# Splits and sums of the next block placed between the additions of the down product, in a one-core streaming trunk layer

## The chip, the core and the metric

The kernel runs on one core of one Trainium2 chip. PE is TensorE, DVE is VectorE, ACT is ScalarE, SP issues the DMAs. Each engine works through its own list of instructions in the order in which they are written, and waits at semaphores for the others. The metric is the device time of one execution in microseconds. All matrix products are made in three matmuls of fp32r pieces: a number is split into a high part (a copy by ACT) and a low part (a difference by DVE), and high x high, high x low and low x high are summed.

## What is computed

One layer for 17 tiles of 128 rows (2048 prompt rows, 128 sample rows), width 1024, d_ff 2816:

```python
h = rms_norm(x, norm1); p = h @ w_in                       # token mixing: gMLP and gated DeltaNet
x = x + jnp.concatenate([y_a, y_b], axis=-1) @ w_o
h2 = rms_norm(x, norm2)
x = x + (jax.nn.silu(h2 @ w_gate) * (h2 @ w_up)) @ w_down
y = rms_norm(x, final_norm)
```

Beside y the layer returns the recurrent states and the last rows of the convolution and of v.

## The kernel before

It has two phases, one program each, with a barrier between them.

**The mixing** (`prompt_phase`) runs tile by tile. Between the small steps of tile t, every engine works off quarters of the large products in step with a common counter (`upto(t, stop)`, with `SLOT` = 32 quarters a tile). Quarter functions also finish the first 12 tiles (`DONE`) as far as the next phase needs them: `scale_rows` (DVE) scales a row tile by its norm, `turn_h2` (PE) transposes its two halves into the bank `gs`, `h2_columns` (DVE) scales them out of PSUM, `store_h2` (SP) stores them. `output(t)` (DVE) forms the mixed tile. At the end SP loads the last weight piece of the next phase (`a["ahead"][-1]`, w_up) into room that row tiles used, stores the state and the last mixed tile, and waits for all of it.

**The feed-forward phase** (`out_phase`) holds three groups of 6, 6 and 5 tiles and runs 11 blocks of 256 columns of d_ff for each: `B` = 0 to 32. Blocks 0, 11 and 22 open a group. Block 10 is called `switch` in the code, block 22 is `BEFORE`. gate and up are computed in a Winograd form of Strassen's algorithm: seven products for each side, 14 in a block (`one_product`, 12 matmuls of 384 or 320 columns each). Their weight pieces go through a ring of five slots: `ring_hi(B, i)` (ACT) and `ring_lo(B, i)` (DVE) split piece i. Four of the seven need sums of quarter blocks, `sum1` to `sum4` (DVE), made in place in `sums`, so sum 2 comes after the pieces of sum 1 have been split. Piece 4 of the next block needs sum 2.

The order of a block's products is A11, S1, S2, S3, A12, A22, S4 (in blocks 0 and 22 A11, A12, S1, S2, S3, A22, S4), each for gate and up. `seed` and `keep_u2` (ACT) carry sums from bank to bank between the products, `keep_p5` saves one. Four results of a block are formed by `corner`, `gate` (ACT), `product`, `out_hi` (ACT) and `out_lo` (DVE).

The down phase follows: 12 (in the last group 10) halves `down_half`, six matmuls of 512 columns each, into four banks in turn. `add_half(B, i)` (DVE) adds half i to `acc`. Half i waits for addition i - 4; half 0 waits for the third `out_lo` of the block. The weights of the down product come as two halves of 512 KB through one buffer: `load_down_half` (SP) waits for `down_half_lo` of the one before.

At the end of a group, `y_factor(gi, t)` (ACT) waits for the additions of tile t and forms its norm, `write_y` (DVE) scales the rows, `store_y` and `load_x` (SP) exchange them for the next group's. At the `switch` the operands of the next group (`operand_hi`, ACT, and `operand_lo`, DVE, seven of 1536 columns) are split between these steps.

Before block 22 comes the output projection of the last group, `last_norms` with `scale_tile`, `turn` (PE), `take_turned` and `early_piece` for its five tiles, and `last_t(i)`, the sums of its operands.

The order of every engine is written out by hand. In the kernel before, the pieces and sums of block B + 1 stand between the four results of block B.

## Time and profile before

| | us |
|---|---|
| median of 3 runs | 2684.31 |
| lowest, highest run | 2680.48, 2686.01 |
| the profiled execution | 2679.19 |
| its span (first to last instruction) | 2677.4 |
| PE busy | 2595.4 |
| DVE busy | 1833.9 |
| ACT busy | 1220.5 |
| DMA, mean | 122 GB/s |

The feed-forward phase begins at 1134.7 us of the span. Read the busy shares first, then who waited for whom on PE, and then the timeline at the places where it waited. A duration in the timeline is that of one instruction; on DVE and ACT the next one may begin a little before the end of the last. In the timeline a block shows neither its number nor the helper's name, only the helper's line: L3090 is `add_half`, L2926 `ring_lo`, L2933 `sum1`, L2938 `sum2`, L2945 `sum3`, L3078 `out_lo`, L2966 and L2962 `operand_lo`, L3129 `take_turned`, L3120 `scale_tile`, L2648 `ring_hi`, L2684, L2688 and L2682 `operand_hi`, L2695 `seed`, L2702 `keep_u2`, L2656 `down_half_hi`, L1171 `h2_columns`, L1399 `scale_rows`.

### The profile page before, as it was taken

The page shows a single profiled execution, that of the slowest core. Times are in us where ns is not written, and L with a number is a line of the kernel's source. Part 1 is how long each engine was busy: PE and PEld are TensorE (multiplying, and loading weights), DVE is VectorE, ACT ScalarE, POOL GpSimd, SP SyncE. Part 2 cuts the span into 40 slices and gives each one's busy share as a digit, 9 for nine tenths or more (in the row PEclk, how much of TensorE's full clock was granted, in tenths as well). Part 3 has the DMA queues.
Part 4 walks back from the last instruction along what each step waited for, and adds up shares of the span by engine and source line. Part 5 has one row for each costly group of instructions (what it writes and reads, how often), then busy time and mean ns, then how long its engine had stood idle before and what let it go on. Part 6 is the DMA issues. An engine that isn't in the chain of part 4 may idle for free.

```text
span 2677.4 us, 47276 instructions
## 1 busy us (share of the span) xinstructions
PE 2595.4 (97%) x18469; PEld 2282.2 (85%) x18469; DVE 1833.9 (68%) x3335; ACT 1220.5 (46%) x2267; POOL 28.1 (1%) x72
## 2 busy tenths in 40 slices
PE   8999999999999999689999999999999998999998
PEld 7878777777787777589999999899999997999997
DVE  4666767677677666587676668667666658677766
ACT  3435655655655656344242436324242435434444
POOL 1000000000000000000000000000000000000000
PEclk9999999999999999899999999999999998999999
DMA  9355444454444547433232325413131251222331
GB/s 310 101 157 174 143 131 131 142 155 115 158 145 117 206 150 245 165 131 114 72 118 71 103 75 186 134 49 94 48 95 48 88 172 48 87 65 86 95 87 56
DMA packets 372255, 325.67 MB, mean 122 GB/s; under 512 B 13985, under 2 KB 314130, under 8 KB 369986
## 3 DMA queue, kind: packets, MB, share of 16 engines
q1 hardware_dynamic: 371650, 322.63, 39.1%
q8 instruction: 148, 2.42, 0.4%
q14 instruction: 73, 0.60, 0.1%
q0 software_dynamic: 384, 0.02, 0.0%
HBM read 261.09 MB, written 61.51 MB: 120 GB/s over the span
## 4 chain that ended last, share of the span: by engine, by line
PE 51%; DVE 4%; ACT 1%; issue 1%; DMA 1%; SPq 0%; DVEq 0%; ACTq 0%
PE down_ps L3316 8%; PE down_ps L3317 8%; PE down_ps L3318 8%; PE up_ps L3322 3%; PE gate_ps L3322 3%; PE up_ps L3321 3%; PE gate_ps L3323 3%; PE gate_ps L3321 3%; PE up_ps L3323 3%; PE down_ps L3322 1%; PE down_ps L3321 1%; PE down_ps L3323 1%; PE gate_ps L3316 1%; PE gate_ps L3318 1%; PE gate_ps L3317 1%; PE up_ps L3317 1%
## 5 line engine op out<-in xcount | busy, mean ns | idle before, releaser
L1673 PE MATMUL pr_p<-hT_hi_p,w_hi_p 128*128 128x512 f32 x992 | 420.0, 423 | 2.1 <-ACT w_in_sb L747 1.1
L1675 PE MATMUL pr_p<-hT_hi_p,w_lo_p 128*128 128x512 f32 x992 | 389.4, 393 | 0.0
L1674 PE MATMUL pr_p<-hT_lo_p,w_hi_p 128*128 128x512 f32 x992 | 389.2, 392 | 0.0
L3090 DVE TENSOR_TENSOR middle<-down_ps,middle 128x512 f32<-128x512 f32 x374 | 257.6, 691 | 174.3 <-PE down_ps L3318 172.0
L3316 PE MATMUL down_ps<-wd_hi,act_hi 128*128 128x512 f32 x748 | 293.0, 392 | 9.8 <-DVE act_lo L3078 9.8
L3317 PE MATMUL down_ps<-wd_lo,act_hi 128*128 128x512 f32 x748 | 292.8, 391 | 0.0
L3318 PE MATMUL down_ps<-wd_hi,act_lo 128*128 128x512 f32 x748 | 292.4, 391 | 0.0
L2926 DVE TENSOR_TENSOR w_ring<-w_in_sb,w_ring 128x512 fp32r<-128x512 f32 x264 | 181.7, 689 | 73.1 <-ACT w_ring L2648 71.2
L1673 PEld LDWEIGHTS pr_p<-hT_hi_p,w_hi_p 128*128 128x128 f32 x992 | 187.2, 189 | 42.2 <-issue 7.2
L1675 PEld LDWEIGHTS pr_p<-hT_hi_p,w_lo_p 128*128 128x128 f32 x992 | 187.0, 189 | 41.7
L1099 DVE TENSOR_TENSOR w_lo_p<-w_in_sb,w_hi_p 128x1024 fp32r<-128x1024 f32 x124 | 150.9, 1217 | 103.9 <-ACT w_hi_p L727 103.6
L2695 ACT ACTIVATE gate_ps<-gate_ps 128x384 f32<-128x384 f32 (+1 forms) x33 | 15.1, 457 | 447.6 <-PE gate_ps L3318 447.6
L1674 PEld LDWEIGHTS pr_p<-hT_lo_p,w_hi_p 128*128 128x128 f32 x992 | 187.7, 189 | 34.8 <-issue 4.3
L2648 ACT ACTIVATE w_ring<-w_in_sb 128x512 fp32r<-128x512 f32 x264 | 165.1, 627 | 47.1 <-PE gate_ps L3323 29.9
L3321 PE MATMUL gate_ps<-h_all,w_ring 128*128 128x384 f32 (+1 forms) x528 | 173.3, 328 | 11.1 <-ACT middle L2702 6.1
L3316 PEld LDWEIGHTS down_ps<-wd_hi,act_hi 128*128 128x128 f32 x748 | 141.1, 189 | 40.0 <-DVE act_lo L3078 11.0
L3321 PE MATMUL up_ps<-h_all,w_ring 128*128 128x384 f32 (+1 forms) x528 | 173.4, 328 | 1.7 <-ACT middle L2702 1.7
L3322 PE MATMUL up_ps<-h_all,w_ring 128*128 128x384 f32 (+1 forms) x528 | 173.0, 328 | 0.0
L3323 PE MATMUL gate_ps<-h_all,w_ring 128*128 128x384 f32 (+1 forms) x528 | 173.0, 328 | 0.0
L3322 PE MATMUL gate_ps<-h_all,w_ring 128*128 128x384 f32 (+1 forms) x528 | 172.9, 327 | 0.0
L3323 PE MATMUL up_ps<-h_all,w_ring 128*128 128x384 f32 (+1 forms) x528 | 172.8, 327 | 0.0
L2926 DVE TENSOR_TENSOR w_ring<-raws,w_ring 128x512 fp32r<-128x512 f32 x198 | 135.9, 686 | 52.8 <-ACT w_ring L2648 52.8
(481 smaller groups left out, 5580.2 us busy)
## 6 DMA issues: line engine op xcount, KB each, us to landing
w_in_sb<-in_w_in SPq DMA_DIRECT2D x100, 512.0 KB, 4.4
raws<-in_w_down SPq DMA_DIRECT2D x66, 512.0 KB, 3.7
w_in_sb<-in_w_gate SPq DMA_DIRECT2D x128, 256.0 KB, 3.1
w_in_sb<-in_w_up SPq DMA_DIRECT2D x128, 256.0 KB, 3.4
stream_tiles<-w_in_sb SPq DMA_DIRECT2D x96, 256.0 KB, 2.5
w_in_sb<-stream_tiles SPq DMA_DIRECT2D x16, 1280.0 KB, 7.5
w_in_sb<-mixed_tiles SPq DMA_DIRECT2D x29, 512.0 KB, 4.8
w_in_sb<-in_w_in SPq DMA_DIRECT2D x5, 2048.0 KB, 15.6
```

Source lines behind the costliest of these rows:

```text
L1673: pe.matmul(out, w_h, x_h, start=start, stop=False)
L1674: pe.matmul(out, w_h, x_l, start=False, stop=False)
L1675: return pe.matmul(out, w_l, x_h, start=False, stop=stop)
L2648: act_e.activation(slot_hi(n), operand_of(role, side), ACT.Copy).then_inc(ring_hi_ready, 1)
L2926: dve.tensor_tensor(slot_lo(n), operand_of(role, side), slot_hi(n).bitcast(F32), ALU.subtract)\
L3090: dve.tensor_tensor(part, half_ps[i % (2 * NH)], part, ALU.add).then_inc(half_added, 1)
L3316: pe.matmul(out, w_h, x_h, start=start, stop=False)
L3317: pe.matmul(out, w_h, x_l, start=False, stop=False)
L3318: return pe.matmul(out, w_l, x_h, start=False, stop=stop)
L3321: pe.matmul(out, w_h, x_h, start=False, stop=True, skip_group_check=True)
L3322: pe.matmul(out, w_h, x_l, start=False, stop=True, skip_group_check=True)
L3323: return pe.matmul(out, w_l, x_h, start=False, stop=True, skip_group_check=True)
```

## The change

In the feed-forward phase, ACT's copies and DVE's splits and sums of the next block move behind the block's last `out_hi` and `out_lo`: `ring_lo(B+1, 0..4)`, `sum1` and `sum2` now stand one by one between additions 0 to 7. This is so in all 31 blocks whose successor is not block 22. In blocks 0 and 22 the seeds move ahead of the third product's neighbours. Around the switch, `write_y(0, 3)`, `(0, 4)` and `(0, 5)` move into block 11, and there `down_half_lo` of the first half and the split of S4 go behind the first `product`. In block 22's opening, `turn(4)` is issued before the first product and two splits go behind `scale_tile(4)`. At the end of the mixing, the last row tile is scaled and turned before the output of the last tile, its two halves go into the two banks `pr` instead of one, and SP stores them last.

```diff
@@ SP, end of the mixing
-            upto(TILES - 1, SLOT + 12)
+            upto(TILES - 1, SLOT + 4)
             sp.wait_ge(row_stored[2], 16 * (DONE // len(rows_of)))
             sp.wait_ge(s["h_ready"], TILES + DONE)
             sp.dma_start(*a["ahead"][-1]).then_inc(s["ahead_loaded"], 16)
...
             store_y(TILES - 1)
+            upto(TILES - 1, SLOT + 12)
@@ DVE, end of the mixing
+                if part == 1 and n == ALL + 1:
+                    scale_rows(TILES + nth(n - 2), rows_of[nth(n - 2) % len(rows_of)])
...
+                turned_in = gs_cols if m < DONE - 1 else pr[i][:].rearrange("p (c i) -> p c i", i=P)
...
+                if t == TILES - 1:
+                    upto(t, SLOT + 2)
                 if t >= 0:
                     output(t)
@@ PE, turn_h2
-                past(pe, s["h2_ready"], turned["h2"])
+                if m < DONE - 1:
+                    past(pe, s["h2_ready"], turned["h2"])
+                    to = gs
+                else:
+                    pe.wait_ge(s["second_added"], DONE)
+                    to = pr[i]
@@ ACT, last_norms and the opening of block 0
                 ring_hi(BEFORE, 4)
+                seed(BEFORE, 0)
                 operand_hi(LAST, S1_T1)
+                seed(BEFORE, 1)
...
+            seed(0, 0)
             operand_hi(0, S1_T1)
+            seed(0, 1)
             ring_hi(0, 4)
@@ ACT, every block
+                late = more
...
-                if more:
+                if more and not late:
                     ring_hi(B + 1, 0)
...
                 out_hi(B, 3)
+                if late:
+                    for i in range(4):
+                        ring_hi(B + 1, i)
                 if more:
                     ring_hi(B + 1, 4)
@@ DVE, last_norms
-                ring_lo(BEFORE, 2)
-                ring_lo(BEFORE, 3)
                 take_turned(2)
+                take_turned(3)
                 scale_tile(4)
                 early_piece_lo(2)
-                take_turned(3)
+                ring_lo(BEFORE, 2)
                 take_turned(4)
                 last_t(0)
+                ring_lo(BEFORE, 3)
@@ DVE, block 11 and every block
                     sum3(B, 0)
                     ring_lo(B, 5)
+                    if B == BLOCKS:
+                        write_y(0, 3)
                     sum3(B, 1)
                     ring_lo(B, 6)
+                    if B == BLOCKS:
+                        write_y(0, 4)
                     ring_lo(B, 7)
                     if B == BLOCKS:
-                        write_y(0, GROUP - 1)
-                    down_half_lo(B, 0)
+                        write_y(0, 5)
+                    else:
+                        down_half_lo(B, 0)
...
                     product(B, 0)
+                    if B == BLOCKS:
+                        operand_lo(1, S4_B22)
+                        down_half_lo(B, 0)
                     ring_lo(B, 12)
...
                 out_lo(B, 3)
+                if late:
+                    add_half(B, 0)
+                    ring_lo(B + 1, 0)
                 add_half(B, 1)
+                if late:
+                    ring_lo(B + 1, 1)
+                    sum1(B + 1, 0)
...
                 for i in range(2, halves_of(B)):
                     add_half(B, i)
+                    if late and i == 2:
+                        sum1(B + 1, 1)
+                    if late and i == 3:
+                        ring_lo(B + 1, 2)
+                    if late and i == 4:
+                        sum2(B + 1, 0)
+                    if late and i == 5:
+                        ring_lo(B + 1, 3)
+                    if late and i == 6:
+                        sum2(B + 1, 1)
+                    if late and i == 7:
+                        ring_lo(B + 1, 4)
                     if switch and i == 4:
                         operand_lo(1, S3_T3)
@@ PE, block 22
                 turn(3)
+                turn(4)
...
-                    if B == BEFORE and i == 0:
-                        turn(4)
```

DVE at the end of the mixing, before and then now. `gs_p` and `pr_p` are the banks that PE turns into, L1399 (now L1403) is `scale_rows`, L1171 (L1175) `h2_columns`, L1586 and L1590 (L1590 and L1594) the output.

```order
1208 L1171 TENSOR_TENSOR w_in_sb<-gs_p,cols 128x512
1209 L1586 SCALAR_TENSOR_TENSOR ya_p<-gb_p,cols,r_p 128x512
1210 L1590 TENSOR_TENSOR w_in_sb<-ya_p,z_p 128x512
1211 L1171 TENSOR_TENSOR w_in_sb<-gs_p,cols 128x512
1212 L1399 TENSOR_SCALAR w_in_sb<-w_in_sb,rstd_p 128x1024
1213 L1171 TENSOR_TENSOR bs_s_p<-gs_p,cols 128x512
1214 L1171 TENSOR_TENSOR h_odd_p<-gs_p,cols 128x512
```

```order
1208 L1175 TENSOR_TENSOR w_in_sb<-gs_p,cols 128x512
1209 L1403 TENSOR_SCALAR w_in_sb<-w_in_sb,rstd_p 128x1024
1210 L1175 TENSOR_TENSOR w_in_sb<-gs_p,cols 128x512
1211 L1590 SCALAR_TENSOR_TENSOR ya_p<-gb_p,cols,r_p 128x512
1212 L1594 TENSOR_TENSOR w_in_sb<-ya_p,z_p 128x512
1213 L1175 TENSOR_TENSOR bs_s_p<-pr_p,cols 128x512
1214 L1175 TENSOR_TENSOR h_odd_p<-pr_p,cols 128x512
```

The scaling moved from behind the output to before it.

ACT at the end of block 10, before and then now. L2648 (now L2659) is `ring_hi`, the table load belongs to the norms, L2752 to L2757 (L2763 to L2768) are the first `y_factor`, L2688 (L2699) the copy of operand S3.

```order
1201 L2742 ACTIVATE act_hi<-middle 128x384
1202 L2648 ACTIVATE w_ring<-raws 128x512
1203 L2733 ACTIVATE middle<-middle 128x384
1204 L2742 ACTIVATE act_hi<-middle 128x384
1205 L2648 ACTIVATE w_ring<-raws 128x512
1206 L2747 ACT_TABLE_LOAD
1207 L2752 ACTIVATE middle,fssum<-middle 128x1024
1208 L2755 ACTIVATE flnv<-fssum,eps_b 128x1
1209 L2757 ACTIVATE frstd<-flnv 128x1
1210 L2688 ACTIVATE h_all<-w_in_sb 128x3x4x128
```

```order
1168 L2753 ACTIVATE act_hi<-middle 128x384
1169 L2659 ACTIVATE w_ring<-w_in_sb 128x512 x2
1170 L2659 ACTIVATE w_ring<-raws 128x512 x3
1171 L2758 ACT_TABLE_LOAD
1172 L2763 ACTIVATE middle,fssum<-middle 128x1024
1173 L2766 ACTIVATE flnv<-fssum,eps_b 128x1
1174 L2768 ACTIVATE frstd<-flnv 128x1
1175 L2699 ACTIVATE h_all<-w_in_sb 128x3x4x128
```

All five copies of the next block's pieces now stand between the last `out_hi` and the table load; before, one did.

DVE in the down phase of block 10, before and then now. L3090 (now L3111) is `add_half`, L2926 (L2947) `ring_lo`, L2959 `sum2`, L2966 (L2987) the split of operand S3, L3037 (L3058) `write_y`.

```order
1662 L3090 TENSOR_TENSOR middle<-down_ps,middle 128x512
1663 L2926 TENSOR_TENSOR w_ring<-raws,w_ring 128x512
1664 L3090 TENSOR_TENSOR middle<-down_ps,middle 128x512 x3
1665 L2966 TENSOR_TENSOR h_all<-w_in_sb,h_all 128x3x4x128
1666 L3090 TENSOR_TENSOR middle<-down_ps,middle 128x512
1667 L3037 SCALAR_TENSOR_TENSOR middle<-middle,frstd,fnorm 128x1024
```

```order
1706 L3111 TENSOR_TENSOR middle<-down_ps,middle 128x512
1707 L2947 TENSOR_TENSOR w_ring<-raws,w_ring 128x512
1708 L3111 TENSOR_TENSOR middle<-down_ps,middle 128x512
1709 L2959 TENSOR_TENSOR raws<-raws,w_in_sb 128x512
1710 L2987 TENSOR_TENSOR h_all<-w_in_sb,h_all 128x3x4x128
1711 L3111 TENSOR_TENSOR middle<-down_ps,middle 128x512
```

Between addition 4 and the split of the operand stands the sum for which ACT's fifth copy waits.

## Rows read from the trace of the kernel before

**Rows 1.** The page, busy time, share of the span and instructions.
```profile
PE 2595.4 (97%) x18469; PEld 2282.2 (85%) x18469; DVE 1833.9 (68%) x3335; ACT 1220.5 (46%) x2267; POOL 28.1 (1%) x72
```
**Rows 2.** Waits of PE: who for whom, total us, times, longest.
```profile
PE gate_ps L3430 <- DVE w_ring L2926: 12.1, 1, 12.1
PE down_ps L3316 <- DVE act_lo L3078: 9.8, 4, 2.7
...
PE gate_ps L3321 <- ACT middle L2702: 6.1, 3, 3.5
PE gate_ps L3321 <- ACT gate_ps L2695: 5.0, 2, 2.6
PE down_ps L3321 <- DVE w_ring L2926: 4.8, 2, 3.5
```
**Rows 3.** Windows, down phases of blocks 10, 11, 22: engines, clock, DMA.
```profile
1638.50:1655.10 16.60, 16.51 (x73) 13.59 (x74) 15.22 (x22) 12.00 (x22) 0.00 (x0) 1.00 0.20 58
1691.80:1709.90 18.10, 18.09 (x73) 14.86 (x74) 11.92 (x19) 1.57 (x3) 0.00 (x0) 0.91 0.00 0
2270.60:2286.10 15.50, 15.42 (x61) 12.61 (x62) 10.29 (x18) 1.49 (x4) 0.00 (x0) 0.89 0.00 1
```
**Rows 4.** Timeline of DVE, block 0: start, us, instruction, idle before.
```profile
1178.28 0.69 DVE L2926 TENSOR_TENSOR w_ring<-w_in_sb,w_ring 128x512 fp32r<-128x512 f32 x1
1178.88 0.69 DVE L2933 TENSOR_TENSOR raws<-w_in_sb 128x512 f32<-128x512 f32 x1
...
1180.63 0.56 DVE L3078 TENSOR_TENSOR act_lo<-middle,act_hi 128x384 fp32r<-128x384 f32 x1
```
**Rows 5.** Timeline of ACT, block 0.
```profile
1157.93 1.49 ACT L2684 ACTIVATE h_all<-middle 128x1536 fp32r<-128x1536 f32 x1 [1.26 <-DVE middle L2994]
...
1160.74 0.48 ACT L2702 ACTIVATE middle<-gate_ps 128x384 f32<-128x384 f32 x1
```
**Rows 6.** Timeline of DVE, then ACT, opening of block 22.
```profile
2234.41 1.23 DVE L3129 TENSOR_TENSOR rest<-down_ps,norm 128x1024 f32<-128x1024 f32 x1 [3.66 <-PE down_ps L3402]
...
2238.49 1.49 DVE L2962 TENSOR_TENSOR h_all<-w_in_sb,h_all 128x1280 fp32r<-128x1280 f32 x1 [0.73 <-ACT h_all L2682]
...
2238.37 0.42 ACT L2695 ACTIVATE gate_ps<-gate_ps 128x320 f32<-128x320 f32 x1
```
**Rows 7.** Timeline of DVE and SP, end of mixing, and its last store's landing.
```profile
1119.23 0.75 DVE L1586 SCALAR_TENSOR_TENSOR ya_p<-gb_p,cols,r_p 128x512 f32<-128x512 f32 x1 [1.09 <-ACT r_p L933]
...
1121.23 0.74 DVE L1399 TENSOR_SCALAR w_in_sb<-w_in_sb,rstd_p 128x1024 f32<-128x1024 f32 x1
...
1125.15 0.69 DVE L1171 TENSOR_TENSOR h_odd_p<-gs_p,cols 128x512 f32<-128x512 f32 x1 [1.27 <-PE gs_p L1889]
...
1126.28 0.38 SPq L629 DMA_DIRECT2D w_in_sb<-in_w_up  x1
...
1127.50 0.45 SPq L552 DMA_DIRECT2D mixed_tiles<-w_in_sb  x1
...
mixed_tiles<-w_in_sb SPq DMA_DIRECT2D x1, 512.0 KB, 5.1
```
**Rows 8.** Timeline of ACT, then DVE, down phase of block 10.
```profile
1642.40 0.62 ACT L2648 ACTIVATE w_ring<-raws 128x512 fp32r<-128x512 f32 x1
...
1645.95 1.47 ACT L2688 ACTIVATE h_all<-w_in_sb 128x1536 fp32r<-128x1536 f32 x1
...
1647.46 1.76 DVE L2966 TENSOR_TENSOR h_all<-w_in_sb,h_all 128x1536 fp32r<-128x1536 f32 x1 [1.02 <-ACT h_all L2688]
```
**Rows 9.** Timeline of ACT and SP, block 11.
```profile
1664.09 0.64 ACT L2648 ACTIVATE w_ring<-w_in_sb 128x512 fp32r<-128x512 f32 x1
...
1667.85 0.48 ACT L2702 ACTIVATE middle<-gate_ps 128x384 f32<-128x384 f32 x1
...
1677.54 0.88 SPq L2479 DMA_DIRECT2D raws<-in_w_down  x1
...
1683.79 1.06 ACT L2656 ACTIVATE wd_hi<-raws 128x1024 fp32r<-128x1024 f32 x1 [6.90 <-DMA raws<-in_w_down]
```

More of the change, by code:

```diff
@@ L1148, in quarter @@
                     conv_tap(n - 2, part + 1)
+                if part == 1 and n == ALL + 1:
+                    scale_rows(TILES + nth(n - 2), rows_of[nth(n - 2) % len(rows_of)])
                 if part == 1 and ITEMS + DONE + 3 <= n < ALL + 3:
                     h2_columns(1, nth(n - 3))
-                if part == 1 and ITEMS + DONE + 2 <= n < ALL + 2:
+                if part == 1 and ITEMS + DONE + 2 <= n < ALL + 1:
                     scale_rows(TILES + nth(n - 2), rows_of[nth(n - 2) % len(rows_of)])
@@ L1886, in turn_h2 @@
                 pe.wait_ge(s["va_ready"], turned["va"])
[L1887 removed]
+                if m < DONE - 1:
[4 more added lines that the diff above has]
+                    to = pr[i]
                 for k in range(4 * i, 4 * i + 4):
[L1889 removed]
+                    last = pe.transpose(to[:, (k % 4) * P:(k % 4 + 1) * P], h2_rows[m % 2][:, k * P:(k + 1) * P], sh["ident"][:])
                 last.then_inc(s["h_turned"], 1)
@@ L2831, in _ @@
                 switch, wo_next = B == BLOCKS - 1, B + 1 == BEFORE
+                late = more
                 if B == BEFORE:
                     last_norms()
-                seed(B, 0)
+                if B not in (0, BEFORE):
+                    seed(B, 0)
                 ring_hi(B, 5)
-                seed(B, 1)
+                if B not in (0, BEFORE):
+                    seed(B, 1)
                 ring_hi(B, 6)
@@ L2889, in _ @@
                 gate21(B)
-                if more:
+                if more and not late:
                     ring_hi(B + 1, 1)
@@ L2893, in _ @@
                 out_hi(B, 2)
-                if more:
+                if more and not late:
                     ring_hi(B + 1, 3)
@@ L3200, in _ @@
                 switch, wo_next = B == BLOCKS - 1, B + 1 == BEFORE
+                late = more
                 opening_t = first_t if B == 0 else last_t
@@ L3262, in _ @@
                 product(B, 1)
-                if more:
+                if more and not late:
                     ring_lo(B + 1, 0)
                 out_lo(B, 1)
-                if more:
+                if more and not late:
                     sum1(B + 1, 0)
@@ L3272, in _ @@
                 product(B, 2)
-                if more:
+                if more and not late:
                     ring_lo(B + 1, 2)
                 out_lo(B, 2)
-                if more:
+                if more and not late:
                     sum2(B + 1, 0)
                 corner12(B, 0)
-                if more:
+                if more and not late:
                     ring_lo(B + 1, 3)
@@ L3283, in _ @@
                 product(B, 3)
-                add_half(B, 0)
+                if not late:
+                    add_half(B, 0)
                 out_lo(B, 3)
+                if late:
+                    add_half(B, 0)
+                    ring_lo(B + 1, 0)
                 add_half(B, 1)
-                if more:
+                if late:
+                    ring_lo(B + 1, 1)
+                    sum1(B + 1, 0)
+                if more and not late:
                     ring_lo(B + 1, 4)
@@ L3302, in _ @@
                         split_mixed(i // 2 - 1)
-                    if b == BLOCKS - 1 and i >= 5 and i % 2 == 1:
+                    if b == BLOCKS - 1 and i >= 5 and i % 2 == 1 and not (switch and i == 11):
                         write_y(gi, (i - 5) // 2)
-                if b == BLOCKS - 1:
+                if b == BLOCKS - 1 and not switch:
                     write_y(gi, groups[gi][1] - 2)
```

5 lines of the change are left out of this document (1 added, 4 removed).

## The prediction

> **What bounds the kernel now.** I read the page first. TensorE is busy for 97% of the span, VectorE for 68%, so only time in which PE stands still can be won [rows 1]. The waits of PE come next, and I placed each wait on the timeline. In 29 of the 33 blocks PE never waits for more than a few hundredths of a microsecond. The waits stand at the end of the mixing, in block 0, around the change of group (blocks 10 and 11), and in the opening of the last group (block 22) [rows 2]. The reader is to see that the ordinary blocks have nothing to give, whatever is moved in them, and that four borders do.
>
> **The ordinary blocks: zero.** 72 matmuls of a down phase take 16.3 us, or 0.227 each, so one half (six matmuls) lasts 1.36 us [rows 3]. VectorE starts a follower 0.60 us after an addition or a split of 512 columns [rows 4]. The moved work puts nine splits and sums between the first additions, so a pair costs 1.20 us against PE's 1.36. By hand, from the start of a down phase: the last `out_lo` at 2.0, addition 0 at 2.5, addition 4 at 7.9, addition 7 at 11.5, split 4 at 12.1. Half 8 starts at 10.9 and needs addition 4, half 11 at 15.0 needs addition 7, and the next block needs split 0 at 16.3. In blocks 2, 4 and 6 a 1.65 us sum is in the way and addition 7 ends at 13.8, still in time. What hides the moved work is the half-empty VectorE of the down phase; if that cover were gone, see the third rival.
>
> **Block 0: -1.8.** PE's down phase waits for the third `out_lo`, which starts at 1180.63 because it stands behind two sums and three splits of the next block; two of these run between 1178.28 and 1179.57 while its product could [rows 4]. Two of the five (1.2 us) delayed the second `out_lo`'s product and difference, the others the third's; the links that stay are product, copy and difference, some 0.55 us each. Run through without the five, the third `out_lo` starts at 1178.85, 1.8 earlier. 1.0 of PE's 2.8 remains. The seeds, moved ahead in this block, return nothing. PE would start the third product at 1144.3 rather than 1146.7, but VectorE's chain of sums and operand splits sets the seventh product (operand ready at 1154.4) and then the ninth: ScalarE's operand copy at 1157.93 waits for VectorE and `keep_u2` follows it at 1160.74 [rows 5]. PE waits there instead. Bounds 0 and -0.5; I take 0.
>
> **The last group's opening (block 22): -5.8, and -0.7 by the clock.** Today the fifth `turn` stands behind the first product, so its rows come at 2234.41, the operand split behind them at 2238.49, and the seed, queued behind that operand's copy, at 2238.37 [rows 6]. Now, with the durations of these rows: `take_turned(2)` 2225.95, `take_turned(3)` 2227.15, `scale_tile(4)` 2228.30, `turn(4)` 2229.1 to 2230.1, `early_piece_lo(2)` done at 2229.7, first product 2230.5 (0.4 later), `take_turned(4)` 2230.4, `last_t` 2231.55, operand copy 2233.1, operand split 2234.4. VectorE's chain is thus 4.1 us early, and from there it alone sets the rest of the block, since PE's ninth product still waits 3.7 us for it. The seed comes at 2232.6, so the third product starts at about 2234.2, where it now waits for a seed that ends at 2238.8. At the down phase the same four instructions leave the chain as in block 0: -1.7. Sum -5.8. Half of the down phases after long waits ran partly at the lower clock: 15.5 us for 60 matmuls, where 13.6 is the full pace [rows 3]. With less waiting before it I give this an even chance to go: -0.7 (between 0 and -1.7).
>
> **The end of the mixing: -4.3.** The last rows are scaled at 1121.23, after the output, though VectorE stood idle before it; PE turns them in two steps around VectorE's copy from one bank, the second copy is at 1125.15, and only then does SP issue the last weight piece at 1126.28 and the last mixed tile at 1127.50, which lands 5.1 us later and lets the next phase begin [rows 7]. Now: scaling at 1118.1, both turns into two banks at 1119.0 to 1120.3, output at 1119.6 and 1120.4 (0.4 later), copies at 1121.1 and 1121.7. SP issues the weights at 1120.1 after the row store, the tile at 1121.2, the two h2 stores at 1121.8 and 1122.4. The limit is then the transfers: 5.1 + 0.4 us of them stood behind 1126.5; two more stores of 0.85 us join them from 1120.5 on, which makes 7.2, so they end at 1127.7 instead of 1132.0: -4.3. Bounds: -6.2 (the shift of the weights' issue) and -3.4 (the shift of the last copies); nearest is the sum of transfers.
>
> **The change of group (blocks 10 and 11): +4.7.** In block 10 the down phase starts without its 2.0 us wait, at 1636.6. But ScalarE's fifth piece copy now waits for a sum that VectorE makes after addition 4, at 1645.1 to 1645.8, and it stands ahead of the table load, the first row factor and the copy of operand S3. Today the piece copy starts at 1642.40 and the copy of S3 3.55 later; now the latter starts at 1645.85 + 3.55 = 1649.4. VectorE waits for it (as it does for 1.02 us today) with seven additions still behind: operand split 1650.9, addition 5 at 1652.6, done 1653.3 [rows 8]. PE's half 9 needs it and was due at 1636.6 + 9 x 1.36 = 1648.8: a new wait of 4.5. Half 10 waits 1.0 more for addition 6, behind `write_y`. Block 11 then starts at 1658.5 instead of 1655.1. In it, `write_y(0, 3)` ahead of the second sum delays ScalarE's copy of that sum from 1664.09 to 1670.5; `keep_u2`, 3.76 behind it, frees PE's seventh product 0.6 later, at 1674.9 instead of 1668.5 and 3.2 after PE could have begun it [rows 9]. `down_half_lo` for the first half, now behind the operand split, ends at 1683.6; SP's load of the second half waits for it, where it was issued at 1677.54 and landed by 1683.79. I take 3.9 to 6.2 us to land, 3.0 from there to the last product, and 3.2 to the down phase: 1693.7 to 1696.0 instead of 1691.8 [rows 3], so +1.9 to +4.2, middle +3.2 with the 2.0 won already inside it.
>
> The granted clock was 0.91 over the down phase of block 11, which followed waits of 3.6 and 2.8 us, and 1.00 over that of block 10, which followed one of 2.0: the first took 18.1 us for what takes 16.3, so a fall to the lower level (1.2 of 2.4 GHz) costs 1.7 us of PE's time [rows 3]. The new waits of 4.5 and 3.2 us can each bring one, partly inside the wait that follows; I add 1.5, between 0 and 3.4.
>
> The Trainium skill (page "TensorE: Matmul & The Clock Gate", Part 1: The HAM clock gate) says that an idle array falls to half rate and that only activity gives the full rate back. The trace agrees with it on block 11 and shows the 2.0 us wait of block 10 without a fall. By that rule each of the two new waits pays in full, which is the second rival's time; by the row of block 10 alone neither would.
>
> **Sum.** -1.8 - 6.5 - 4.3 + 4.7 = -7.9, say -8. The profiled execution took 2679.2 (span 2677.4 and 1.8 around it), which makes 2671.2; the median of the three runs is 5.1 above the profiled one, so against it the forecast is 2684.3 - 8 = 2676.3.
>
> **Rivals.** First, the change of group loses nothing: the operand copy comes early enough for addition 5. For it speaks that VectorE has 1.0 us of slack there today; against it the 3.4 us by which ScalarE's queue is held. Then the 2.0 stay won: -1.8 - 6.5 - 4.3 - 2.0 = -14.6, 2669.7. Second, the clock: the waits of 4.5 and 3.2 us, and the one in block 22, each bring two stretches like the one of block 11, and 5 us more go: -3, 2681.3. Third, slower: VectorE does not hold 1.20 us for a pair in the down phase. It decides from 1.36 on; at 1.42, nine pairs put the additions 0.5 us behind in each of the 31 blocks with the new order, and with all four banks full PE waits for that: +15.5 - 8 = +7.5, 2691.8. Against it stand all rows of splits and additions, none of which follows later than 0.69. Fourth, the change does not do what it says at the end of the mixing: the transfers land as late as before, as the last stores now queue behind weights, tile and state. Then -8 + 4.3 = -3.7, 2680.6.
>
> **How the numbers follow.** Forecast 0.50 (2673 to 2679), first rival 0.17, second 0.15, third 0.08, fourth 0.10. A measurement of this kernel can tell about 0.2%, 5.4 us, from no change. Faster by more: 0.45 + 0.17 + 0.03 + 0.02 = 0.67. Slower: 0.08. The same: 0.25. The range from 2667 to 2683 takes in the forecast, the first rival with the larger bounds of block 22 and the mixing, and the second and fourth, and leaves out the third.
>
> **What would show it.** Right: PE idle inside block 10's down phase before half 9, with VectorE waiting about 5 us for ScalarE's operand copy; the third product of block 22 some 3.7 us after its first, where it was 8.8; the next phase starting near 1130.4; no waits in ordinary blocks. Wrong: a down phase of an ordinary block longer than 16.4 us, the seventh product of block 11 without a wait, or a copy of S3 near 1646.

## Result and profile after

The changed kernel takes 2667.23 us, the median of five runs (2665.88 to 2671.52). The kernel before, beside it on the same chip, takes 2681.67 (2676.64 to 2686.01, five runs). The ratio is 0.995, 95% interval 0.9932 to 0.9967, about 13 us faster. The profiled execution took 2671.52 with a span of 2669.8, which is 7.6 us below the span of before. One execution, of the eleven with the old end of the mixing below, took 4159.02 us at a mean granted clock of 0.571; it enters no ratio and no reading here.

To place the gain I cut both timelines at points that every version has: the last state updates of the mixing, ACT's first copy of the feed-forward phase, and the first matmul of each down product. I did the same with a second profiled execution of the changed kernel. It differs from the first in where the clock was low and, between blocks 9 and 12, in how long one load took (see the last rows of this section).

| stretch | before | after, first profile | second | change | forecast |
|---|---|---|---|---|---|
| start to last state updates | 1117.20 | 1120.09 | 1118.04 | +2.9, +0.8 | 0 |
| to first copy of the next phase | 17.47 | 13.07 | 12.73 | -4.4, -4.7 | -4.3 |
| to the down product of block 0 | 46.56 | 44.77 | 44.70 | -1.8, -1.9 | -1.8 |
| block 0 to block 9 | 409.68 | 409.64 | 409.65 | 0.0 | 0 |
| block 9 to block 12 | 148.08 | 151.56 | 149.53 | +3.5, +1.5 | +4.7 |
| block 12 to block 21 | 409.56 | 409.56 | 409.56 | 0.0 | 0 |
| block 21 to block 23 | 162.09 | 154.32 | 156.26 | -7.8, -5.8 | -6.5 |
| block 23 to the end | 366.78 | 366.81 | 366.79 | 0.0 | 0 |

The first line aside, the stretches sum to -10.5 and -11.0, where the forecast was -7.9. The first line is code that both kernels share, and its +2.9 in the first profile is not the change's: in twelve profiles this code took from 1114.2 to 1120.3.

Busy times first, to be held against [rows 1]. PE has the same work and is busy for the same time (a matmul at the lower clock counts as busy for longer), so in this pair of profiles the shorter span is time in which PE stood still:

```profile
PE 2595.2 (97%) x18469; PEld 2281.8 (85%) x18469; DVE 1817.5 (68%) x3335; ACT 1221.4 (46%) x2267; POOL 28.1 (1%) x72
```

The waits of PE in the changed kernel (who for whom, total us, times, longest), beside [rows 2]. The waits for `out_lo` at the starts of down products fell from 9.8 to 2.6, the wait of the third products for ACT's seed (5.0) is no longer among the large ones, and a new wait for `add_half` (L3111) has come:

```profile
PE gate_ps L3478 <- DVE w_ring L2947: 12.8, 1, 12.8
...
PE gate_ps L3368 <- ACT middle L2713: 6.7, 2, 3.9
PE down_ps L3363 <- DVE middle L3111: 4.5, 2, 4.2
PE down_ps L3368 <- DVE w_ring L2947: 4.5, 3, 2.4
...
PE down_ps L3363 <- DVE act_lo L3099: 2.6, 3, 0.9
```

The same three down products as in [rows 3], of blocks 10, 11 and 22 (stretch, length, busy PE, PEld, DVE, ACT and POOL, granted clock, DMA share, GB/s). Those of 11 and 22 had a clock of 0.91 and 0.89 and have 1.00 now. That of block 10 has lost 4 us of PE's busy time to a wait:

```profile
1633.20:1649.80 16.60, 12.48 (x56) 9.99 (x54) 10.60 (x18) 9.84 (x17) 0.00 (x0) 1.00 0.03 11
1693.40:1709.90 16.50, 16.41 (x72) 13.58 (x73) 14.26 (x25) 4.00 (x7) 0.00 (x0) 1.00 0.01 1
2264.60:2280.00 15.40, 15.39 (x72) 13.00 (x73) 13.91 (x24) 3.89 (x7) 0.00 (x0) 1.00 0.01 1
```

Block 0, where [rows 4] had a split and a sum ahead of the third `out_lo`. The third `out_lo` now follows its product with only ACT's copy between:

```profile
1176.18 0.55 DVE L3092 TENSOR_TENSOR middle<-up_ps,middle 128x384 f32<-128x384 f32 x1
1177.32 0.56 DVE L3099 TENSOR_TENSOR act_lo<-middle,act_hi 128x384 fp32r<-128x384 f32 x1 [0.59 <-ACT act_hi L2753]
```

The end of the mixing (DVE, then SP), to be read against [rows 7]: the scaling of the last rows at 1120.95 stands behind the state updates and one column copy, the output comes after it, and SP issues the weights and the mixed tile ahead of the last two stores:

```profile
1120.95 0.74 DVE L1403 TENSOR_SCALAR w_in_sb<-w_in_sb,rstd_p 128x1024 f32<-128x1024 f32 x1
...
1122.45 0.74 DVE L1590 SCALAR_TENSOR_TENSOR ya_p<-gb_p,cols,r_p 128x512 f32<-128x512 f32 x1
...
1124.44 0.68 DVE L1175 TENSOR_TENSOR h_odd_p<-pr_p,cols 128x512 f32<-128x512 f32 x1
...
1122.98 0.38 SPq L629 DMA_DIRECT2D w_in_sb<-in_w_up  x1
...
1124.22 0.45 SPq L552 DMA_DIRECT2D mixed_tiles<-w_in_sb  x1
```

What lands last has changed with it. Before, it was the mixed tile (issued at 1127.50, landed 5.1 us later, at 1132.6, and the next phase began 2.1 later). Now it is the last of the two stores, which SP issues at 1125.23 and which lands 5.8 us later, at 1131.1, again 2.1 before the next phase. The view of the DMAs in this window (KB each, us from issue to landing):

```profile
mixed_tiles<-w_in_sb SPq DMA_DIRECT2D x1, 512.0 KB, 5.6
...
h_tiles<-h_odd_p SPq DMA_DIRECT2D x1, 256.0 KB, 5.8
```

The opening of block 22 (DVE, then ACT), against [rows 6]: `take_turned` of the fifth tile, the operand's split and the first seed, which were at 2234.41, 2238.49 and 2238.37:

```profile
2230.11 1.23 DVE L3150 TENSOR_TENSOR rest<-down_ps,norm 128x1024 f32<-128x1024 f32 x1
...
2234.20 1.49 DVE L2983 TENSOR_TENSOR h_all<-w_in_sb,h_all 128x1280 fp32r<-128x1280 f32 x1
...
2232.17 0.42 ACT L2706 ACTIVATE gate_ps<-gate_ps 128x320 f32<-128x320 f32 x1 [3.45 <-PE gate_ps L3365]
```

The down product of block 10 (ACT, DVE, then PE), against [rows 8]. ACT's piece copy, table load and first row factor stand in front of the copy of operand S3, DVE waits 5.09 us for that copy where it waited 1.02, and PE's half 9 waits 4.23 us for the addition behind it:

```profile
1642.44 0.63 ACT L2659 ACTIVATE w_ring<-raws 128x512 fp32r<-128x512 f32 x1 [1.77 <-DVE raws L2959]
1643.09 1.28 ACT L2758 ACT_TABLE_LOAD   x1
...
1646.00 1.47 ACT L2699 ACTIVATE h_all<-w_in_sb 128x1536 fp32r<-128x1536 f32 x1
...
1647.50 1.76 DVE L2987 TENSOR_TENSOR h_all<-w_in_sb,h_all 128x1536 fp32r<-128x1536 f32 x1 [5.09 <-ACT h_all L2699]
...
1649.91 0.50 PE L3363 MATMUL down_ps<-wd_hi,act_hi 128*128 128x512 f32 x1 [4.23 <-DVE middle L3111]
```

Block 11 (SP, then ACT), against [rows 9]: the load of the second half of the down matrix is issued at 1681.51 and ACT waits for it until 1687.28.

```profile
1681.51 0.37 SPq L2490 DMA_DIRECT2D raws<-in_w_down  x1
...
1687.28 1.06 ACT L2667 ACTIVATE wd_hi<-raws 128x1024 fp32r<-128x1024 f32 x1 [8.04 <-DMA raws<-in_w_down]
```

In the second profile the same load is used 3.7 us after its issue and not 5.8:

```profile
1679.14 0.37 SPq L2490 DMA_DIRECT2D raws<-in_w_down  x1
...
1682.87 1.06 ACT L2667 ACTIVATE wd_hi<-raws 128x1024 fp32r<-128x1024 f32 x1 [6.01 <-DMA raws<-in_w_down]
```

PE's stop in front of block 11's last product, which waits for this load, is 2.6 us in the first profile and 0.6 in the second. That is the whole difference between +3.5 and +1.5 in the table.

### The profile page after: what moved, and what is told of

The parts are those of the page before. It is cut to its first block, busy times and chain, and to the rows that moved or that the text cites. A ratio compares the mean times of both kernels' runs of the same rounds, so it can differ in the third digit from the quotient of the medians.

```text
span 2669.8 us, 47276 instructions
## 1 busy us (share of the span) xinstructions
PE 2595.2 (97%) x18469; PEld 2281.8 (85%) x18469; DVE 1817.5 (68%) x3335; ACT 1221.4 (46%) x2267; POOL 28.1 (1%) x72
## 4 chain that ended last, share of the span: by engine, by line
PE 52%; DVE 3%; ACT 1%; issue 1%; DMA 1%; DVEq 0%; ACTq 0%
PE down_ps L3363 8%; PE down_ps L3364 8%; PE down_ps L3365 8%; PE gate_ps L3368 3%; PE gate_ps L3370 3%; PE gate_ps L3369 3%; PE up_ps L3368 3%; PE up_ps L3370 3%; PE up_ps L3369 3%; PE down_ps L3370 1%; PE down_ps L3368 1%; PE down_ps L3369 1%; PE gate_ps L3363 1%; PE gate_ps L3365 1%; PE gate_ps L3364 1%; PE up_ps L3363 1%
## 5 line engine op out<-in xcount | busy, mean ns | idle before, releaser
L3111 DVE TENSOR_TENSOR middle<-down_ps,middle 128x512 f32<-128x512 f32 x374 | 254.6, 683 | 41.6 <-PE down_ps L3365 41.6
L2947 DVE TENSOR_TENSOR w_ring<-w_in_sb,w_ring 128x512 fp32r<-128x512 f32 x264 | 181.3, 687 | 64.9 <-ACT w_ring L2659 63.0
L2659 ACT ACTIVATE w_ring<-raws 128x512 fp32r<-128x512 f32 x198 | 124.4, 629 | 180.4 <-DVE raws L2954 96.8
L2659 ACT ACTIVATE w_ring<-w_in_sb 128x512 fp32r<-128x512 f32 x264 | 161.5, 625 | 37.2 <-PE gate_ps L3370 31.2
L2947 DVE TENSOR_TENSOR w_ring<-raws,w_ring 128x512 fp32r<-128x512 f32 x198 | 135.1, 682 | 55.2 <-ACT w_ring L2659 55.2
```

Source lines behind the costliest of these rows:

```text
L2659: act_e.activation(slot_hi(n), operand_of(role, side), ACT.Copy).then_inc(ring_hi_ready, 1)
L2947: dve.tensor_tensor(slot_lo(n), operand_of(role, side), slot_hi(n).bitcast(F32), ALU.subtract)\
L3111: dve.tensor_tensor(part, half_ps[i % (2 * NH)], part, ALU.add).then_inc(half_added, 1)
```

## Experiments

**The changed kernel once more.**

> The changed kernel itself, on the same chip and in the same rounds as its variants. My theory: the change wins at the borders alone, about 4.4 us at the end of the mixing, 1.8 in block 0 and 6 to 8 in block 22, and loses 3 to 5 at the change of group, so 8 to 10 us net; what the medians show beyond that (14) is how much of each run stood at the lower granted clock, so over the runs the time falls by about half of the time spent at the lower level. Rival: the ordinary blocks win as well, 5 us in all, and the net gain is 13 us at the same granted clock.

No edit. Measured: 2666.05 us (five runs), the kernel before 2679.19 (16 runs), ratio 0.9952 (0.9939 to 0.9966). It gave the second profile of the table. The result repeats, and no ordinary block has gained: the stretches sum to -11.0, a little over the 8 to 10 that I had expected.

**The ordinary blocks.** Two runs take the new order out of them, first with the list of three blocks, then with four.

```diff
-                late = more
+                late = more and B in (0, BLOCKS - 1, BEFORE)
```

> The new order only in blocks 0, 10 and 22; the 28 other blocks have the old one. My theory: within 2 us of the changed kernel, and every ordinary block is as long in the trace as before (45.4 us with 384 columns). Rival (ordinary blocks win 0.2 us each): 5 us slower than the changed kernel.

Measured: 2670.72, ratio 0.997 (0.9958 to 0.9981), 4.7 us slower than the changed kernel beside it, where I had expected at most 2. Block 0 to block 9, block 12 to 21 and block 23 to the end took 409.65, 409.56 and 366.79, the same to 0.01 us. The loss stood between blocks 9 and 12, 153.73 instead of 149.53. The list had left out block 11, which is no ordinary block: there PE waits at the down product's start. So I ran the list with block 11 in it.

```diff
-                late = more
+                late = more and B in (0, BLOCKS - 1, BLOCKS, BEFORE)
```

> The new order of pieces and sums in the down products of blocks 0, 10, 11 and 22 only (the earlier run had it in 0, 10 and 22); all ordinary blocks from 1 to 9, 12 to 20 and 23 to 31 in the old order. Theory (the ordinary blocks give nothing; what the run with three blocks lost stood at the start of block 11's down product, whose first half waited there for the activations behind the pieces, as before the change): the time of the changed kernel, within 1 us, near 2666, and the step from block 11's down product to block 12's at 45.6 us and not 47.2. Rival (the ordinary blocks give a little each through the clock, and the three-block run showed it): 4 to 5 us slower than the changed kernel, near 2671.

Measured: 2667.79 (0.996, 0.9946 to 0.9973), beside 2678.34 for the kernel before. From the first copy of the feed-forward phase to the end it takes 1536.53 us, where the changed kernel takes 1536.50 and the run before it 1540.09. The rows of PE's waits for `out_lo`, first of the list of three, then of the list of four:

```profile
PE down_ps L3363 <- DVE act_lo L3099: 3.5, 2, 2.7
```

```profile
PE down_ps L3363 <- DVE act_lo L3099: 2.0, 3, 0.9
```

The wait of 2.7 us is back in the first and gone in the second. With it come 1.7 us of the step from block 11 to 12 (47.26 against 45.60), the low clock of [rows 3]. The new order is worth nothing in 27 blocks and 3.6 us in block 11.

**The change of group in the old order** (blocks 10 and 11, with `write_y`, `down_half_lo` and the split of S4 where they had been; block 11's own down product keeps the new order).

```diff
-                late = more
+                late = more and not switch
...
-                    if B == BLOCKS:
-                        write_y(0, 3)
                     sum3(B, 1)
                     ring_lo(B, 6)
-                    if B == BLOCKS:
-                        write_y(0, 4)
...
```

> Blocks 10 and 11 in the old order, all else as changed. My theory: 3 to 5 us faster than the changed kernel; the waits of 4.4 and 0.7 us inside block 10's down phase and of 2.9 us before block 11's seventh product are gone, those of 2.0 before block 10's down phase, 3.6 before block 11's last product and 2.8 before its down phase are back. Rival (the change of group costs nothing in sum, since its new waits only take the place of the old ones): no difference.

Measured: 2663.31 (0.9942, 0.993 to 0.9955), 2.7 us faster than the changed kernel beside it. Block 9 to block 12 took 146.09, against 149.53 for the changed kernel and 148.08 for the one before: the new order costs 3.4 to 5.5 there. By medians it is 2.7, a little under the 3 to 5 that I had expected, and single executions of the two kernels overlap. Of the waits that I had expected, the new ones are gone and the stops of 2.0 us at block 10's down product and of 3.6 in front of block 11's last product are back. The 2.8 us at the start of block 11's down product did not come back, because the new order stayed there. The rival, no difference, fell.

**The end of the mixing in the old order.**

```diff
-            upto(TILES - 1, SLOT + 4)
+            upto(TILES - 1, SLOT + 12)
...
             store_y(TILES - 1)
-            upto(TILES - 1, SLOT + 12)
...
-                if t == TILES - 1:
-                    upto(t, SLOT + 2)
...
```

> The end of the mixing in the old order, all else as changed. My theory: 4.4 us slower than the changed kernel, and the time from the last state update of the mixing to the first instruction of the feed-forward phase is 4.4 us longer. Rival (the transfers end as late in either order): no difference.

Measured: 2671.75 (0.9972, 0.9963 to 0.9981), 5.7 slower than the changed kernel. From the last state updates to the next phase it took 17.65 us, against 12.73. SP issued the mixed tile behind all stores:

```profile
1123.17 0.32 SPq L490 DMA_DIRECT2D h_tiles<-bs_s_p  x1
1125.13 0.32 SPq L490 DMA_DIRECT2D h_tiles<-h_odd_p  x1
1125.55 0.38 SPq L629 DMA_DIRECT2D w_in_sb<-in_w_up  x1
...
1126.76 0.45 SPq L552 DMA_DIRECT2D mixed_tiles<-w_in_sb  x1
```

**The openings of blocks 0 and 22 in the old order.**

```diff
-                seed(BEFORE, 0)
                 operand_hi(LAST, S1_T1)
-                seed(BEFORE, 1)
...
-            seed(0, 0)
             operand_hi(0, S1_T1)
-            seed(0, 1)
...
+                ring_lo(BEFORE, 2)
+                ring_lo(BEFORE, 3)
                 take_turned(2)
-                take_turned(3)
                 scale_tile(4)
...
                 turn(3)
-                turn(4)
...
                     one_product(B, i)
+                    if B == BEFORE and i == 0:
+                        turn(4)
```

> The changed kernel with the old openings of blocks 0 and 22: the seeds behind the opening's operand again, the pieces of block 22 ahead of the turned rows, and the last turn behind the first product; the new order in the down products and at the mixing's end stays. Theory (block 22's opening gives 5.8 to 6.5, block 0's seeds 0): the step from block 21's down product to block 22's goes from 116.0 to 117.0 back to about 122 us; from the start of the network to block 0's down product 44.6 us stays; in all 5 to 7 us slower than the changed kernel, near 2672. Rival (the seeds in block 0 give the 1.8 us there, the down product's order nothing): 46.4 us from the network's start to block 0's down product, in all 7 to 9 slower. Rival (block 22's gain is the clock's and not the order's): under 3 us.

Measured: 2671.16 (0.9973, 0.9964 to 0.9983), 3.4 slower than the run with the list of four beside it. To the down product of block 0 it took 44.59 us, as with the new opening (44.59 to 44.77): the seeds give nothing there, and the 1.8 us belong to the down product's order. Block 21 to block 23 took 158.69. So of the changed kernel's 5.8 to 7.8 the order ahead of the down product gives 3.4 (from 162.09), and the opening only 2.4 to 4.4. Up to the down product alone (120.34 us from block 21's to block 22's, against 122.11 before and 115.93 and 117.04 changed) the order gives 1.8 and the opening 3.3 to 4.4, for 1.7 and 4.1 in the prediction; the rest is clock. The size that I had written for this run (5 to 7) was too large, because it gave the opening what the down product's start brings. ACT's operand copy and the seed queued behind it are back in their old order:

```profile
2232.44 1.27 ACT L2693 ACTIVATE h_all<-w_in_sb 128x1280 fp32r<-128x1280 f32 x1 [7.71 <-DVE w_in_sb L3036]
2233.62 0.42 ACT L2706 ACTIVATE gate_ps<-gate_ps 128x320 f32<-128x320 f32 x1
```

**The copy of operand S3 first.** The one step that the forecast of the 4.5 us wait rests on.

```diff
                 if late:
                     for i in range(4):
                         ring_hi(B + 1, i)
+                        if switch and i == 1:
+                            operand_hi(1, S3_T3)
...
-                        if switch and t == 1:
-                            operand_hi(1, S3_T3)
```

> The changed kernel with one step moved on ScalarE: the big part of the second group's operand for the third product is made behind the first two pieces of block 11, ahead of the third piece, and not behind the first row factor. Theory (half 9 of block 10's down product waits 4.4 us because VectorE stands for 5.1 us in front of this operand): the stall of 4.4 us at half 9 goes, but VectorE then has sums and row outputs back to back, and 0.7 to 1.5 us of it is late again at the last halves; 3 to 4 us faster than the changed kernel, near 2663, with 57 us in place of 58 to 60 from block 10's down product to block 11's. Rival (VectorE is full there and this wait only names the last of many): under 1.5 us faster, with stalls of the halves behind VectorE's additions that sum to over 3 us.

Measured: 2663.00 (0.9946, 0.9933 to 0.9959), 4.8 us faster than the run with the list of four beside it by medians; block 10 to block 11 took 55.03 us instead of 58.36. The timeline of ACT, DVE and PE: the copy stands right behind the first two pieces, and DVE takes it without a wait. Half 9 no longer waits. What is left is a wait of 1.04 us at half 10, for addition 6, which stands behind the first row output:

```profile
1629.99 1.48 ACT L2699 ACTIVATE h_all<-w_in_sb 128x1536 fp32r<-128x1536 f32 x1
...
1636.16 1.75 DVE L2987 TENSOR_TENSOR h_all<-w_in_sb,h_all 128x1536 fp32r<-128x1536 f32 x1
...
1639.96 1.28 DVE L3058 SCALAR_TENSOR_TENSOR middle<-middle,frstd,fnorm 128x1024 f32<-128x1024 f32 x1 [0.85 <-ACT frstd L2768]
1641.17 0.68 DVE L3111 TENSOR_TENSOR middle<-down_ps,middle 128x512 f32<-128x512 f32 x1
...
1641.90 0.50 PE L3363 MATMUL down_ps<-wd_hi,act_hi 128*128 128x512 f32 x1 [1.04 <-DVE middle L3111]
```

The place in ACT's queue was the cause of the wait at half 9. The wait that is left is another one: DVE itself waits 0.85 us there for the row factor from ACT, and then has the row output (1.28 us) ahead of the addition.

**And the row outputs out of the way of the sums.** This run has the edit of the run before it as well. Of the row outputs, `write_y(0, 3)` and `(0, 4)` had moved into block 11 with the change; `(0, 5)` stood there already.

```diff
-                    if B == BLOCKS:
-                        write_y(0, 3)
                     sum3(B, 1)
...
-                    else:
-                        down_half_lo(B, 0)
+                    down_half_lo(B, 0)
...
-                        down_half_lo(B, 0)
...
-                    if b == BLOCKS - 1 and i >= 5 and i % 2 == 1 and not (switch and i == 11):
+                    if b == BLOCKS - 1 and i >= 5 and i % 2 == 1:
                         write_y(gi, (i - 5) // 2)
```

The last change puts `write_y(0, 3)` back into block 10's down product.

> As the run with the third sum's operand first, and in block 11 no row output stands between the two third sums: output 3 goes back into block 10's down product, outputs 4 and 5 stand behind the seventh and eighth piece, and half 0 of the down matrix is split where it was before the change. Theory (the 2.9 us in front of block 11's seventh product and the 2.6 us in front of its last come from the row outputs ahead of the sums and from the late half): both waits fall under 1 us each, another 3 to 5 us, near 2659 and so as fast as or faster than the kernel with blocks 10 and 11 in the old order (2663). Rival (the row outputs only move, and delay the third sums from block 10 instead): within 1.5 us of the run before it.

Measured: 2660.13 (0.9936, 0.9924 to 0.9949), 2.9 faster than the run before it by medians, of which the stretch from block 9 to 12 shows 1.0 (145.33 after 146.34). The theory held for the seventh product alone, by half: PE's stop in front of it, start to start over the usual distance, fell from 3.0 to 1.8 us. The stop in front of the last product grew from 1.6 to 3.3. The row outputs were not what it waits for: the load of the down matrix's second half, issued at 1668.11, landed 7.1 us later here, and 4.7 us after its issue in the run before.

**The load of the second half.** In the kernel with the old change of group (block 11, SP, ACT and PE), the load stands behind an input row and four weight pieces, and the product that needs a ring slot behind its split waits:

```profile
1664.94 0.32 SPq L2542 DMA_DIRECT2D middle<-row_tiles  x1
1665.31 0.43 SPq L2484 DMA_DIRECT2D w_in_sb<-in_w_gate  x1
...
1667.44 1.00 SPq L2490 DMA_DIRECT2D raws<-in_w_down  x1
...
1673.91 1.06 ACT L2667 ACTIVATE wd_hi<-raws 128x1024 fp32r<-128x1024 f32 x1 [6.89 <-DMA raws<-in_w_down]
...
1676.88 0.69 PE L3362 MATMUL down_ps<-h_all,w_ring 128*128 128x384 f32 x1 [3.48 <-DVE w_ring L2947]
```

One issue in SP's program is moved, in this kernel and in the one with the row outputs out of the way:

```diff
-                if not (gi == 0 and b == BLOCKS - 1):
+                if not (gi == 0 and b == BLOCKS - 1) and B != BLOCKS:
                     load_down_half(NH * B + 1)
...
                     for t in range(GROUP + 1):
                         if t < GROUP:
                             store_y(t, 0)
+                        if t == GROUP - 1:
+                            load_down_half(NH * (B + 1) + 1)
                         if t > 0:
                             load_x(t - 1, 1)
```

> The kernel with blocks 10 and 11's change of group in the old order (2663.3), and in SP's queue the second half of block 11's down matrix stands ahead of the last two input rows and of block 12's first pieces. Theory (the 3.6 us that PE waits in front of block 11's last product come from this load, issued at 1667.4 behind four pieces and landed 6.5 us later, though its buffer was free at 1657.9): the load is issued near 1660 and landed near 1665, the wait of 3.6 us goes, and the step from block 10's down product to block 11's falls from 52.2 to between 48.5 and 49.5 us; 3 to 4 us faster than without it, near 2660. Rival (the last product waits as long for something that stands behind the load, a piece of block 11 or ScalarE's queue): under 1 us.

> The same move of the load of block 11's second half in the kernel with the row outputs around the sums (2660.1), where the wait in front of the last product was 3.3 us. Theory: 2.5 to 3.3 us faster than that one, near 2657.3, with 51 us from block 10's down product to block 11's; since that kernel has 1.9 us of waits in block 10's down phase which the old order has not, and saves 1.9 us at its start, the two should come out within 1.5 us of each other. Rival: VectorE, with five row outputs and the sums, is late for the last product anyway, and at least 2 of the 3.3 us stay.

Measured: 2656.51 (0.9921, 0.9907 to 0.9935) and 2655.85 (0.9922, 0.9909 to 0.9936), beside 2678.53. The stretch from block 9 to 12 takes 139.62 and 140.74, that is 6.5 and 4.6 less than without the move. In the first of the two, SP issues the load at 1660.45 and ACT takes it in turn, without a wait for the DMA:

```profile
1660.45 0.43 SPq L2490 DMA_DIRECT2D raws<-in_w_down  x1
...
1669.01 1.04 ACT L2669 ACTIVATE wd_hi<-raws 128x1024 fp32r<-128x1024 f32 x1
```

The wait in front of the last product is gone in both, and in the first also a stretch of 6.8 us at the lower clock, which stood at this wait, at 1676 (hence more than I had expected). These two kernels beat the one before by 22 us, and the changed one, which was not run beside them, by some 10 (medians).

## Why the prediction was right, point by point

The forecast was 2676.3 in a range from 2667 to 2683, and faster the likeliest. The time, 2667.2, is inside by 0.2 us, and the number alone would speak for the first rival (2669.7), which fell. By mechanism the change came out nearly as written; that the time is still in the range is in part luck. The distance of 9 us has three parts.

- **Ordinary blocks, 0.** Right to 0.05 us over 27 blocks, and shown by taking the new order out of them. DVE holds 1.20 us a pair; the third rival fell.
- **Block 0, -1.8.** Measured -1.8 to -2.0, all of it the down product's start. The seeds gave nothing, as taken: shown by the run without them.
- **Block 22, -5.8 and -0.7.** In the first profile everything up to the down product came to -6.2 and the clock in it to -1.6 (rows above, 0.89 to 1.00), in the second -5.1 and -0.8. My steps for DVE and ACT are met within 0.4 us (seed 2232.17 for 2232.6, operand split 2234.20 for 2234.4; the down product of block 21 stands at the same time in both kernels to 0.1). The term is right; it was split wrongly only in the expectation of the experiment.
- **End of the mixing, -4.3.** Measured -4.4 to -4.9, and +4.9 when undone. The fourth rival fell. The size is right, the way to it not quite: I had charged the two stores behind the tile with 1.7 us more of transfers, and the tile landed 5.6 us after its issue (5.1 before), half a microsecond more. But I had the tile land last, and it is the second store that lands last now, 1.3 us behind the tile (rows above).
- **Change of group, +4.7.** The two waits are there as worked out: 4.4 us in front of half 9 (4.5 forecast) and 2.9 in front of the seventh product (3.2), measured start to start; half 10 lost 0.7 (1.0). The operand copy stands 12.8 us behind the start of the down product, as forecast (1636.6 to 1649.4). The copy itself stands at 1646.00, a place that I had named as a sign of being wrong; but the down product begins 3.3 us earlier than I had it, and DVE's wait of 5.09 us is there, so it is no such sign. Counted from the down product of block 9, block 11's starts 5.0 us later than before in the first profile and 3.1 in the second, where I had +3.2 and +1.5 of clock. The load decides between the two: 5.8 and 3.7 us from issue to use, for my bounds of 6.2 and 3.9. It was issued 1.3 us later than worked out. In the run with the old end of the mixing, where the clock did not fall after the seventh product's wait, it was issued 1.1 us earlier than in the first profile, so this part is the clock's, and 1.5 was about right for it. What failed is a term for the clock that I left out. I added what the new waits could cost and did not credit what the wait at the start of block 11's down product had cost so far: the 1.7 us that I read in [rows 3] came back, 47.20 to 45.6 us for the step to block 12. So the border came to +3.5 and +1.5. The first rival, that nothing is lost there, fell: undoing it is worth 2.7 us by medians.
- **The second rival, the clock.** It fell too. The first profile has low clock at blocks 10 and 11 (stretches of 3.4 us at 1651 and 1671; in the second 6.8 at 1645 and 3.4 at 1669), but over the whole execution the lower level lasted 54.9 us, before 62.6. Most of that difference, 6.8 us (20.5 before, 13.7 after), stands around the barrier between the phases, where PE is busy for 7.3 of the 20.5 us, and is worth nothing here: with 20.5 us of it in the run with the old end of the mixing, the way to block 0's down product took the same 44.6 us. The Trainium skill ("TensorE: Matmul & The Clock Gate", Part 1: The HAM clock gate) says that an idle array falls to half rate. By that rule both new waits pay. In both profiles of the changed kernel each has its stretch of low clock beside it. But the wait of 1.8 to 2.0 us at block 10's down product has none, in the kernel before or in the run with the old order there, and in the run with the old end of the mixing the seventh product's wait, 3.0 us, has none either. A wait of this size pays in one execution and not in the next.

So the first part of the distance is the terms themselves: -10.5 and -11.0 for -7.9. The second part is the yardstick. I set the forecast from the median of three runs, 2684.31, which was 5.1 above the profiled execution. Five runs gave 2681.67, and 38 later ones of the same kernel a median of 2678.7.

The third is the difference between one profile and the median. The profiled execution of the changed kernel was its slowest of five, with 2.9 us more in a part that the change leaves alone. (It took 2671.5, and for it I had 2671.2; these agree by luck, as the 2.9 us made up for a gain that was 2.6 larger than forecast.) The window from 100 to 150 us of the span, before and after, shows where (columns as above):

```profile
100.00:150.00 50.00, 50.00 (x277) 43.29 (x276) 27.57 (x55) 13.93 (x27) 1.63 (x2) 0.93 0.34 92
```

```profile
100.00:150.00 50.00, 50.00 (x258) 43.60 (x257) 25.08 (x46) 13.16 (x24) 1.58 (x1) 0.86 0.30 80
```

PE never rests in either, and the changed kernel gets 19 matmuls less done at a clock of 0.86. The stretches sum to -10.5 and -11.0 in the two profiles of the changed kernel, and to -11.1 in the run with the list of four. Over many runs the median span fell by 12.3 (2676.9 in the 38 later ones of before, 2664.6 in the ten of the changed kernel). That last microsecond has no place in a profile, and I leave it open.

## What to carry to other kernels

Work that is moved behind an urgent step pays only where that step is the last to arrive: here at the starts of four down products out of 33. At each border ask of every queue that the moved work passes what stands behind it, and where an old wait goes, credit the clock that it had cost as well as charging the new waits. And when a wait only changes its place as the work in front of it is moved, follow it to the DMA: one load that stood behind rows and weight pieces for others was worth 4.6 to 6.5 us, as much as the largest single reordering of the engines (4.4 to 4.9, the end of the mixing).

## What the runs showed of the hardware

The granted clock falls at the same places of the mixing, near 130 us in all twelve profiles and near 1077 in seven, but for different times, and the mixing's length goes with it. The twelve profiles, by the length of the low stretches that begin near 130 and near 1077 us:

| near 130 | near 1077 | to the last state updates, us |
|---|---|---|
| 6.8 | 0 | 1114.2, 1114.5, 1115.0, 1115.2 |
| 6.8 | 3.4 | 1116.5, 1116.6, 1116.7, 1117.2 |
| 10.2 | 0 | 1117.3 |
| 10.2 | 3.4 | 1118.0 |
| 13.7 | 3.4 | 1120.1, 1120.3 |

Between the means of neighbouring rows, 3.4 us more at 1.2 in place of 2.4 GHz go with 0.7 to 2.6 us more of the mixing, and in all the same code differs by up to 6 us. That is nearly half of what the change brings: the profiled pair alone would have said -7.6, and only stretches between common points, or medians of many runs, say -11 to -12.

What follows a wait of PE differs in the same way. The 2 us wait of block 10's down product brought no fall of the clock in the three profiles that have it. The 4.4 us wait in front of half 9 brought a stretch of 3.4 us in three profiles and of 6.8 in three others. The wait of about 3 us in front of block 11's seventh product brought one in six profiles and none in a seventh (the old end of the mixing), and a wait of 3.3 us in front of block 11's last product brought one there and none in the run with the row outputs moved.

The load of 512 KB for block 11's second half took from 3.7 to 7.7 us from issue to landing in the twelve profiles.
